# A hybrid decoder layer on one core: the sample's dilated attention and SSD moved into the output projection's Block

## The chip, the cores and the metric

The kernel runs on one core of a Trainium2 chip, as one launch. The metric is the device time of that core in microseconds (us), the median of several runs. Everything is float32; matrix products are made of three passes over a high and a low part of each operand.

## What is computed

One layer for a prompt of 2048 tokens and for a sample of 8 sequences with one new token each; both share the weights. Each token is projected, mixed by three mixers side by side, projected out with `w_out` and sent through a gated feed-forward part:

```python
def layer(x, rel_bias, ln_mix_w, w_in, ..., past=None):
    aq, ak, av, bq, bk, bv, logf, cz, cxbc, cdt = in_project(rmsnorm(x, ln_mix_w), w_in, fgate_b)
    ...
    a_out, win_new = dilated_decode(aq, ak, av, win_bufs, rel_bias)     # sample; dilated_prompt for the prompt
    b_out = fox_decode(bq, bk, bv, logf, fox_kv, fox_logf, page_table)
    c_out, h_new, conv_new = ssd_mixer(cz, cxbc, cdt, conv_buf, h0, conv_w, conv_b, dt_bias, A_log, D_skip, ssm_norm_w)
    x = x + jnp.concatenate([a_out, b_out, c_out], axis=-1) @ w_out
    f, ffn_new = conv_ffn(rmsnorm(x, ln_ffn_w), ffn_buf, w_up, ffn_conv_w, ffn_conv_b, w_down)
```

For the sample, the dilated attention has three groups of two heads. Each attends from one token to 128 cached rows at distance d, 2d, ... (d = 1, 4, 16) and to itself; the groups are merged by a softmax over their log-sums. The sample's SSD is a four-tap convolution, a silu, and for each head a state update `h = h * exp(dt*A) + (x*dt) B`, with `y = C h + D x`, a gate and an RMSNorm.

## The kernel before

`program` runs stages one after the other, each a Block of its own: all five engines meet at its end, and no engine starts the next stage earlier. The order is `project`, `fox_stage` (FoX attention of prompt and sample), `local_stage` (dilated attention and SSD of the prompt), `dilated_decode`, `ssd_decode` (the sample's), `out_project`, `channel_mixer`, `finish`. Between some of them `clear_semaphores` gives semaphores back. Inside a Block each engine runs its own list in order, and semaphores tie the lists together.

**`dilated_decode`** (line 2349) loads all own rows and all cache rows, then VectorE works through the groups (lines 2421 to 2432), GpSimd takes one maximum over all partitions (line 2407), ScalarE the exponentials, TensorE the sums over partitions with a matrix of ones (line 2474). SP stores one row and four statistics for each group to `ma` (line 2398).

**`ssd_decode`** (line 2479) puts the 8 sequences on 8 partitions for the convolution, writes B and C to memory and reads them back as twelve broadcasts over 64 partitions each (line 2543, `sd_bc`), updates the state in three parts (lines 2600 to 2607), stores it and writes a row to `mc`.

**`out_project`** (line 1538) takes 17 tiles of 128 tokens: tile 0 is the sample, tiles 1 to 16 are the prompt. It splits the eight chunks of `w_out` into high and low parts through two buffers, and computes for all tiles the shares of the dilated groups and the SSD's norm (lines 1735 to 1747). For each tile, SP loads the mix in three pieces from `ma`, `mb`, `mc` into one of two buffers (lines 1622 to 1624) and `x` (line 1627). GpSimd multiplies it by norm, weights and shares (lines 1657 to 1661). TensorE turns it in by 8 transposes (line 1810), ScalarE and VectorE split it (lines 1687, 1756), TensorE makes 48 products (lines 1836 to 1838) and turns the normalized previous tile out by 8 transposes (line 1817). VectorE adds the residual (line 1766), ScalarE and VectorE make the RMSNorm (square, root, three Newton operations, scale), VectorE weighs the result (line 1780, in the listings `op_h`), and ScalarE's queue stores `x2` and `h2` (lines 1693, 1702). The tiles run in a hardware loop of two tiles a trip (`over_pipeline`, line 1522); SP loads the mix of tile t+1 once tile t is turned in and its predecessor's residual is added:

```python
                    sp.wait_ge(m_turned, t + 1)
                    load(t + 1, 1 - slot)
                    sp.wait_ge(x2_ready, t + 1)
                    load_x(t + 1, 1 - slot)
```

Here `m_turned`, `x2_ready` start one ahead. `channel_mixer` begins with the load of `h2` (line 1970).

## Time and profile before

| | us |
|---|---|
| median of 3 runs | 3397.13 |
| lowest, highest | 3391.59, 3399.49 |
| the profiled execution | 3402.59 |
| its span, first to last instruction | 3399.9 |
| mean granted TensorE clock, share of full | 0.947 |

The profile records one execution. Its times count from the first instruction, and its pages name instructions by line, engine, operation and the tiles written and read. PE is TensorE, PEld its weight load, DVE VectorE, ACT ScalarE, POOL GpSimd, SP the engine that issues most DMAs (SPq its DMA issues, ACTq ScalarE's). Over the span TensorE is busy for 3028.7 us (89%), VectorE for 1605.9 (47%), ScalarE for 878.2 (26%), GpSimd for 757.8 (22%). The stages around the change are at these times: the dilated attention of the sample from 1409.57, its SSD from 1475.42, the output projection from 1546.79, the channel mixer from 1842.49.

### The profile page before, as it was taken

Reading aid. Unit: us, or ns where it says so; the run is one execution under the profiler, and the core shown is the slowest. Engines: PE = TensorE matmul, PEld = TensorE weight load, DVE = VectorE, ACT = ScalarE, POOL = GpSimd, SP = SyncE. Lnnn points to the kernel's source line nnn. Section 1 sums busy time; section 2 is a strip of 40 time slices with the busy share of each in tenths; the row PEclk is TensorE's granted clock in tenths of the full one; section 3 lists DMA queues with packets and bytes.
Section 4 is the critical chain, followed back from the end, with each engine's and each line's share of the span. In section 5 each row is a group of like instructions: output and inputs, shape, how many; then the busy total and the mean of one; then the engine's idle time right before and its main releaser. Section 6 shows DMA issues by size and latency. Waiting matters only on the chain. (4 is left out here: it accounts for less than half of the span.)

```text
span 3399.9 us, 45796 instructions
## 1 busy us (share of the span) xinstructions
PE 3028.7 (89%) x16539; PEld 2604.6 (77%) x16539; DVE 1605.9 (47%) x2952; ACT 878.2 (26%) x1647; POOL 757.8 (22%) x547
## 2 busy tenths in 40 slices
PE   8999999689998899413885999999999899999998
PEld 6888889677675899303774999999999788888886
DVE  5013211257775888443333455544555544444445
ACT  4223222233332455202222221112211322112212
POOL 4002100234442455201211112211221112211220
PEclk9999999889999999756997999999999999999999
DMA  4454325557762333434444311111111511111101
GB/s 152 169 205 163 103 91 173 136 167 207 200 193 89 91 91 98 122 67 122 142 147 182 111 37 59 53 37 37 44 56 50 186 37 50 61 38 37 62 25 51
DMA packets 227573, 352.16 MB, mean 104 GB/s; under 512 B 73502, under 2 KB 161175, under 8 KB 221448
## 3 DMA queue, kind: packets, MB, share of 16 engines
q1 hardware_dynamic: 221601, 310.06, 29.9%
q0 software_dynamic: 944, 22.61, 1.8%
q10 hardware_dynamic: 4896, 17.83, 1.3%
q8 instruction: 71, 1.16, 0.1%
q14 instruction: 61, 0.50, 0.0%
HBM read 285.64 MB, written 93.95 MB: 112 GB/s over the span
## 5 line engine op out<-in xcount | busy, mean ns | idle before, releaser
L2985 PE MATMUL pj_acc<-pj_w_hi,pj_h_hi 128*128 128x480 f32 (+5 forms) x952 | 356.6, 375 | 8.5 <-DVE pj_w_lo L2885 8.5
L2986 PE MATMUL pj_acc<-pj_w_lo,pj_h_hi 128*128 128x480 f32 (+5 forms) x952 | 355.6, 374 | 0.0
L2987 PE MATMUL pj_acc<-pj_w_hi,pj_h_lo 128*128 128x480 f32 (+5 forms) x952 | 354.9, 373 | 0.0
L2314 PE MATMUL cm_g_ps<-cm_h_hi,cm_up_hi 128*128 128x344 f32 (+1 forms) x880 | 310.0, 352 | 36.8 <-DVEq L2258 30.7
L2077 POOL TENSOR_TENSOR cm_dn_lo<-cm_dn_raw,cm_dn_hi 128x1024 fp32r<-128x1024 f32 x44 | 107.8, 2472 | 1000.5 <-ACT cm_dn_hi L2119 1000.5
L2314 PE MATMUL cm_u_ps<-cm_h_hi,cm_up_hi 128*128 128x344 f32 (+1 forms) x880 | 309.5, 352 | 2.7 <-DVE cm_a_lo L2218 2.7
L2316 PE MATMUL cm_g_ps<-cm_h_hi,cm_up_lo 128*128 128x344 f32 (+1 forms) x880 | 309.5, 352 | 0.0
L2316 PE MATMUL cm_u_ps<-cm_h_hi,cm_up_lo 128*128 128x344 f32 (+1 forms) x880 | 308.8, 351 | 0.0
L2315 PE MATMUL cm_g_ps<-cm_h_lo,cm_up_hi 128*128 128x344 f32 (+1 forms) x880 | 308.7, 351 | 0.0
L2315 PE MATMUL cm_u_ps<-cm_h_lo,cm_up_hi 128*128 128x344 f32 (+1 forms) x880 | 308.2, 350 | 0.0
L2885 DVE TENSOR_TENSOR pj_w_lo<-pj_w_raw,pj_w_hi 128x480 fp32r<-128x480 f32 (+3 forms) x112 | 76.3, 703 | 393.8 <-ACT pj_w_hi L2840 393.8
L2072 POOL TENSOR_TENSOR cm_up_lo<-cm_up_raw,cm_up_hi 128x2048 fp32r<-128x2048 f32 x44 | 205.0, 4659 | 193.9 <-ACT cm_up_hi L2099 193.9
L2182 DVE TENSOR_SCALAR cm_conv<-cm_gate,cm_small 128x344 f32<-128x344 f32 (+2 forms) x110 | 54.2, 493 | 334.7 <-ACT cm_gate L2112 192.4
L2314 PEld LDWEIGHTS cm_g_ps<-cm_h_hi,cm_up_hi 128*128 128x128 f32 x880 | 166.7, 189 | 53.3 <-issue 31.1
L371 POOL TENSOR_TENSOR fp_prod<-fp_kv,fp_q_own 128x1024 f32<-128x1024 f32 x64 | 151.4, 2366 | 226.9 <-DVE fp_s_dec L414 226.9
L2985 PEld LDWEIGHTS pj_acc<-pj_w_hi,pj_h_hi 128*128 128x128 f32 (+1 forms) x952 | 175.2, 184 | 34.3 <-issue 9.0
L2987 PEld LDWEIGHTS pj_acc<-pj_w_hi,pj_h_lo 128*128 128x128 f32 (+1 forms) x952 | 174.8, 184 | 25.7 <-issue 1.1
L2986 PEld LDWEIGHTS pj_acc<-pj_w_lo,pj_h_hi 128*128 128x128 f32 (+1 forms) x952 | 174.7, 183 | 24.9 <-issue 0.5
L2232 DVE TENSOR_TENSOR cm_y<-cm_y,cm_y_ps 128x1024 f32<-128x1024 f32 x99 | 120.9, 1221 | 137.5 <-PE cm_y_ps L2341 137.5
L2818 ACT ACTIVATE pj_row<-pj_acc,pj_rstd 128x480 f32<-128x480 f32 (+6 forms) x119 | 76.2, 641 | 409.0 <-PE pj_acc L2987 374.4
L2314 PEld LDWEIGHTS cm_u_ps<-cm_h_hi,cm_up_hi 128*128 128x128 f32 x880 | 165.9, 189 | 18.6 <-DVE cm_a_lo L2218 3.1
L2315 PEld LDWEIGHTS cm_g_ps<-cm_h_lo,cm_up_hi 128*128 128x128 f32 x880 | 166.6, 189 | 16.5
(431 smaller groups left out, 6538.0 us busy)
## 6 DMA issues: line engine op xcount, KB each, us to landing
fp_kv<-in_fox_kv SPq DMA_DIRECT2D x256, 256.0 KB, 3.0
cm_up_raw<-in_w_up SPq DMA_DIRECT2D x44, 1024.0 KB, 4.9
cm_dn_raw<-in_w_down SPq DMA_DIRECT2D x44, 512.0 KB, 3.5
out_s_win<-in_cache POOLq DMA_DIRECT2D x8, 2047.0 KB, 9.3
proj_a<-pj_row SPq DMA_DIRECT2D x48, 240.0 KB
sp_raw<-proj_b SPq DMA_DIRECT2D x16, 640.0 KB, 4.1
pj_w_raw<-in_w_a SPq DMA_DIRECT2D x10, 960.0 KB, 8.0
dp_raw<-proj_a SPq DMA_DIRECT2D x48, 192.0 KB, 3.4
```

What stands on the lines that cost most here:

```text
L371: pool.tensor_tensor(prod[:, n % 2], kv[:, at:at + QUART, 0], q_own[:, a // 2:a // 2 + 1].to_broadcast([P, QUART, F]), ALU.mult).then_inc( ...
L2072: pool.tensor_tensor(up_lo[:, s], up_raw[:, s], up_hi[:, s].bitcast(F32), ALU.subtract).then_inc(up_ready, 1)
L2077: pool.tensor_tensor(dn_lo[:, s], dn_raw[:, s], dn_hi[:, s].bitcast(F32), ALU.subtract).then_inc(dn_ready, 1)
L2232: v.tensor_tensor(y[:, n], y[:, n], sums(H, n).rearrange("p a n -> p (a n)"), ALU.add).then_inc(added, 1)
L2314: pe.matmul(out, hi, h_hi[:, k, cs], start=(k == 0), stop=False)
L2315: pe.matmul(out, hi, h_lo[:, k, cs], start=False, stop=False)
L2316: last = pe.matmul(out, lo, h_hi[:, k, cs], start=False, stop=(k == KT - 1))
L2818: act.activation(row[0:m, n % ROWS, 0:wide], acc[0:m, n % BANKS, 0:wide], ACT.Copy, scale=rstd[0:m, t:t + 1]).then_inc(evac, 1)
L2885: v.tensor_tensor(w_lo[:, j % 2, k, 0:n], w_raw[:, k, 0:n], w_hi[:, j % 2, k, 0:n].bitcast(F32), ALU.subtract).then_inc(w_ready, 1)
L2985: pe.matmul(out, h_hi[:, k, place(t)], w_hi[:, j % 2, k, 0:wide], start=(k == 0), stop=False)
L2986: pe.matmul(out, h_hi[:, k, place(t)], w_lo[:, j % 2, k, 0:wide], start=False, stop=False)
L2987: last = pe.matmul(out, h_lo[:, k, place(t)], w_hi[:, j % 2, k, 0:wide], start=False, stop=(k == KT - 1))
```

## The change

`dilated_decode`, `ssd_decode` and `over_pipeline` go. `out_project` becomes `out_stage`, one Block without a hardware loop, that also does the sample's two mixers. The semaphores are cleared between `local_stage` and `out_stage`.

- The tiles are written out in the order 1 to 16 and then 0. A *slot* is the piece of the program in which TensorE multiplies one tile: slot s has tile number s in that order, counted from 0; slots 0 and 1 are done together at the start, with the weight chunks as they come. A slot is divided by phases 1 to 9, and a step of the sample's work has an address `at(slot, phase)`. Each engine has two generators of steps (`dilated`, `ssd`) that it advances at its `until(slot, phase)`.
- There are three mix buffers and three weight buffers, and the mix of tile s+2 is loaded in slot s. Turn-in, split, turn-out and weighing are done in halves of four chunks. GpSimd uses the shares directly and makes three operations for a tile, without the two copies.
- All transfers of the stage are issued by SP, the stores of `x2` and `h2` too.
- The dilated groups are done one after the other with one set of buffers, from slots 2, 5 and 8 on, with one all-reduce each (three for one); the own rows are read as two broadcasts of 128 columns for each group, the own V as one row. The next group's loads wait for the store of the last group's result.
- The SSD's convolution runs on 128 partitions (16 for each sequence, 56 columns) after 26 small loads; all of it goes to memory and x comes back from there. The broadcasts go to two buffers: eight are issued in slot 5, four in slot 9. The state update runs in slots 7 to 12.
- The shares and norm of tile 0 are made at the end of slot 13, after the sample's results were stored.

```diff
+    ORDER = list(range(1, ALL_TILES)) + [0]
+    def group_slot(g):
+        return 2 + 3 * g
+    state_at = [[(7, 5), (7, 7), (7, 9), (8, 9), (9, 3)],
+                [(9, 5), (9, 9), (10, 3), (10, 5), (10, 7)],
+                [(11, 3), (11, 5), (11, 7), (11, 9), (12, 3)]]
...
         @block.sync
+            def load_mix(j):
+                if j >= 3:
+                    sp.wait_ge(m_turned, 2 * (j - 2))
...
+            def dilated():
+                for g in range(GROUPS):
+                    if g:
+                        yield at(group_slot(g) - 1, 9)
+                        sp.wait_ge(d_added, 2 * g)
+                        sp.wait_ge(d_stored, 32 * g)
+                    for k in range(2):
+                        sp.dma_start(d_own[:, :, k], bcast(pa.tensor, k * A_WIDTH + g * P, [[COLS_A, DEC], [1, P]])
+                                     ).then_inc(d_landed, 16)
+                    sp.dma_start(d_row[:], ...).then_inc(d_landed, 16)
+                    sp.dma_start(d_kv[:].rearrange("p b k c -> p b (k c)"), ...).then_inc(d_landed, 16)
+                    yield at(group_slot(g) + 2, 9)
+                    sp.wait_ge(d_added, 2 * g + 2)
+                    sp.dma_start(ma[0:DEC, g * P:(g + 1) * P]..., d_row[:]).then_inc(d_stored, 16)
...
+            load_w(0)
+            sp.dma_start(c_sum[:, 1:], ...).then_inc(sums_in, 16)
+            load_mix(0)
...
+            for s in range(1, N + 1):
+                until(s, 4)
+                if 3 <= s + 2 < LAST:
+                    load_mix(s + 2)
+                if s == SAMPLE_SLOT:
+                    sp.wait_ge(d_stored, 32 * GROUPS)
+                    sp.wait_ge(s_out, 16 * (XT + 3))
...
+                    load_mix(LAST)
+                if s >= 2:
+                    for j in residuals(s):
+                        sp.wait_ge(x2_ready, j + 1)
+                        sp.dma_start(x2_d[t * P:(t + 1) * P, :], x2[:, j % 2]).then_inc(x2_stored[j % 2], 16)
+                        if j + 2 < N:
+                            load_x(j + 2)
+                until(s, 6)
+                    for j in norms(s):
+                        sp.wait_ge(h2_ready, 2 * j + 2)
+                        sp.dma_start(h2_d[ORDER[j]], h2[:, j % 2]).then_inc(h2_stored[j % 2], 16)
+                until(s, 9)
...
         @block.gpsimd
+            for j in range(3):
+                mixing(j)
+            for s in range(1, N):
+                if 3 <= s + 2 < N:
+                    mixing(s + 2)
+                beside.until(at(s, 9))
...
         @block.vector
+            for s in range(2, N + 1):
+                for j in residuals(s):
+                    residual(j)
+                if s + 1 < N:
+                    split(s + 1, 0)
+                for n, j in enumerate(norms(s)):
+                    scale(j)
+                    if n == 0:
+                        until(s, 4)
+                        if s + 1 < N:
+                            split(s + 1, 1)
+                        until(s, 6)
+                    weigh(j, 0)
+                    until(s, 7)
+                    weigh(j, 1)
+                until(s, 9)
+                if s == SAMPLE_SLOT:
+                    factors_of(0, 1, 2)
...
         @block.tensor
+            for s in range(2, N):
+                if s + 1 < N:
+                    turn_in(s + 1, 0)
+                until(s, 1)
+                pe.wait_ge(m_ready, 2 * s + 2)
+                pe.wait_ge(x2_ready, s - 1)
+                multiply(s, 0, range(0, 4))
+                if s + 1 < N:
+                    turn_in(s + 1, 1)
+                until(s, 2)
+                multiply(s, 0, range(4, 8))
+                until(s, 5)
...
+                multiply(s, 1, range(0, 4))
+                if s != 3:
+                    turn_out(ends[-1], 0)
+                until(s, 8)
+                multiply(s, 1, range(4, 8)).then_inc(mm_done, 1)
...
+                turn_out(ends[-1], 1)
+                until(s, 9)
```

Three places in the engines' lists. The first is SP's DMA issues of one tile in the projection's loop (`mix_a`, `mix_b`, `mix_c` are the pieces of the mix, `op_x` the residual's input), before:

```order
L1622 DMA op_mix<-mix_a 128x384
L1623 DMA op_mix<-mix_b 128x256
L1624 DMA op_mix<-mix_c 128x384
L1627 DMA op_x<-in_x 128x1024
L1525 REGISTER_ALU
L1525 COMPARE_AND_BRANCH
```

and now, at the end of slot 4 and the start of slot 5 (`h` is the store of `h2`, `x` that of `x2`):

```order
L1790 DMA h<-op_h 128x1024
L1693 DMA mix_a<-dd_row 8x1x128
L1695 DMA mix_a<-dd_stat 8x1x4
L1685 DMA dd_own<-proj_a 128x8x128 x2
L1687 DMA dd_row<-proj_a 1x8x128
L1689 DMA dd_kv<-in_cache 128x8x256
L1718 DMA conv_rows<-sd_conv 128x56
L1659 DMA op_mix<-mix_a 128x384
L1660 DMA op_mix<-mix_b 128x256
L1661 DMA op_mix<-mix_c 128x384
L1783 DMA x<-op_x 128x1024
L1666 DMA op_x<-in_x 128x1024
```

Two stores and five transfers of the sample now stand ahead of the mix load of tile 7 (with a wait between the stores and the loads). The second place is VectorE's tile work in the loop, from the end of one tile's norm to the next tile's residual, before:

```order
L1519 TENSOR_TENSOR op_rstd<-op_rstd,op_tmp 128x1
L1780 TENSOR_TENSOR op_h<-op_tr_ps,op_lnw 128x1024
L1755 REGISTER_ALU
L1756 TENSOR_TENSOR op_m_lo<-op_in_ps,op_m_hi 128x1024
L1766 TENSOR_TENSOR op_x<-op_acc_ps,op_x 128x1024
L1769 TENSOR_SCALAR op_sq<-op_sq 128x1
```

and now in slot 5:

```order
L1519 TENSOR_TENSOR op_rstd<-op_rstd,op_tmp 128x1
L1990 TENSOR_TENSOR dd_prod<-dd_kv,dd_own 128x1024
L1923 TENSOR_TENSOR op_m_lo<-op_in_ps,op_m_hi 128x512
L1992 TENSOR_REDUCE dd_s<-dd_prod 128x16
L1977 TENSOR_TENSOR op_h<-op_tr_ps,op_lnw 128x512
L1994 SCALAR_TENSOR_TENSOR dd_s<-dd_s,dd_bias 128x16
L1998 TENSOR_TENSOR dd_prod<-dd_own 128x1024
L1977 TENSOR_TENSOR op_h<-op_tr_ps,op_lnw 128x512
```

The group's first product, which needs the cache rows, stands between the norm and both the second split and the first weighing. The third place is GpSimd around the sample's all-reduce (`dd_m`; a bare `ISA` is an instruction without named tiles), before:

```order
L2407 ISA dd_m<-dd_s 128x48
L2353 UNCONDITIONAL_BRANCH
L1645 UNCONDITIONAL_BRANCH
L1653 COPY op_share_now<-op_share 128x6
L1655 COPY op_c_now<-op_c_rstd 128x1
L1657 ISA
L1657 TENSOR_TENSOR op_mix<-op_mix,op_c_now 128x384
```

and now in slots 2 and 3:

```order
L1810 TENSOR_TENSOR op_mix<-op_mix,op_share 128x384
L1816 ISA
L1816 ISA dd_m<-dd_s 128x16
L1806 ISA
L1806 TENSOR_TENSOR op_mix<-op_mix,op_c_rstd 128x384
L1807 TENSOR_TENSOR op_mix<-op_mix,op_norm_w 128x384
```

The bare instruction ahead of a mix's first multiplication stood once, behind the one all-reduce; now it stands behind each of three, in the middle of the tiles, and not at the start of the stage.

## Rows read from the trace of the kernel before

**Rows 1.** Busy time by stretch; columns: stretch, length, engines (instructions), granted clock, DMA share, GB/s.
```profile
1409.50:1475.40 65.90, 9.66 (x22) 5.03 (x22) 26.94 (x33) 0.38 (x2) 0.50 (x1) 0.58 0.36 122
1475.40:1546.80 71.40, 1.90 (x12) 1.25 (x12) 33.70 (x37) 2.28 (x6) 0.00 (x0) 0.50 0.50 94
1600.00:1815.00 215.00, 192.46 (x932) 156.30 (x932) 68.12 (x149) 51.97 (x74) 40.90 (x70) 1.00 0.41 142
```

**Rows 2.** Timeline of both sample stages: start, length, engine, line, [idle before <- releaser].
```profile
1409.57 0.35 SPq L2388 DMA_DIRECT2D dd_ones<-in_consts  x1
...
1436.31 1.87 PE L2463 MATMUL dd_den_ps<-dd_rel,dd_onehot 32*128 32x6 f32 x8 [36.08 <-DMA dd_kv<-in_cache]
...
1473.37 0.62 SPq L2400 DMA_DIRECT2D mix_a<-dd_stat  x1
...
1475.42 0.36 SPq L2524 DMA_DIRECT2D sd_ident<-in_consts  x1
...
1491.23 1.08 DVE L2572 TENSOR_TENSOR sd_tmp<-sd_past,sd_taps 8x896 f32<-8x896 f32 x1
...
1503.62 12.46 SPq L2543 DMA_DIRECT2D sd_bc<-bc_rows  x12
...
1523.20 1.23 DVE L2600 TENSOR_TENSOR sd_upd<-sd_bc,sd_col 128x1024 f32<-128x1024 f32 x1 [18.18 <-DMA sd_bc<-bc_rows]
...
1544.44 0.30 SPq L2551 DMA_DIRECT2D mix_c<-sd_y  x1
```

**Rows 3.** DMA issues of the dilated stage and the projection: count, KB each, median us to landing.
```profile
dd_kv<-in_cache SPq DMA_DIRECT2D x3, 1024.0 KB, 18.9
...
dd_ones<-in_consts SPq DMA_DIRECT2D x1, 64.0 KB, 1.8
...
op_stats<-mix_a SPq DMA_DIRECT2D x1, 102.0 KB, 5.6
...
op_c_sum<-mix_c SPq DMA_DIRECT2D x1, 8.5 KB, 6.5
```

**Rows 4.** Timeline of the start of the output projection.
```profile
1546.79 0.84 SPq L1612 DMA_DIRECT2D op_w_raw<-in_w_out  x2
...
1550.70 1.06 ACT L1669 ACTIVATE op_w_hi<-op_w_raw 128x1024 fp32r<-128x1024 f32 x1 [6.28 <-DMA op_w_raw<-in_w_out]
...
1557.48 0.20 DVE L1735 TENSOR_TENSOR op_top<-op_stats 128x34 f32<-128x34 f32 x1 [2.58 <-DMA op_lnw<-in_ln_ffn]
...
1558.55 1.28 ACT L1675 ACT_TABLE_LOAD   x1
...
1561.76 0.18 DVE L1519 TENSOR_TENSOR op_c_rstd<-op_c_rstd,op_c_tmp 128x17 f32<-128x17 f32 x1
...
1569.05 0.82 POOL L1657 TENSOR_TENSOR op_mix<-op_mix,op_c_now 128x384 f32<-128x384 f32 x1 [6.73 <-issue]
...
1569.94 1.96 POOL L1658 TENSOR_TENSOR op_mix<-op_mix,op_norm_w 128x384 f32<-128x384 f32 x1
```

**Rows 5.** Timeline of one tile of the output projection's loop.
```profile
1611.78 1.09 PE L1810 MATMUL op_in_ps<-op_ident,op_mix 128*128 128x128 f32 x8 [1.82 <-POOL op_mix L1661]
...
1615.19 1.22 DVE L1766 TENSOR_TENSOR op_x<-op_acc_ps,op_x 128x1024 f32<-128x1024 f32 x1
...
1618.82 0.36 SPq L1624 DMA_DIRECT2D op_mix<-mix_c  x1
...
1623.12 0.19 POOL L1653 COPY op_share_now<-op_share 128x6 f32 x1 [11.39 <-DMA op_mix<-mix_c]
...
1623.91 1.03 PE L1817 MATMUL op_tr_ps<-op_ident,op_xn 128*128 128x128 f32 x8
...
1626.33 1.09 PE L1810 MATMUL op_in_ps<-op_ident,op_mix 128*128 128x128 f32 x8 [1.39 <-POOL op_mix L1661]
```

**Rows 6.** Timeline of the projection's end and the channel mixer's first load.
```profile
1830.07 1.22 DVE L1766 TENSOR_TENSOR op_x<-op_acc_ps,op_x 128x1024 f32<-128x1024 f32 x1
...
1842.49 0.33 SPq L1970 DMA_DIRECT2D cm_y<-h  x1
```

More of the change, by code:

```diff
@@ L1665, in _ @@
+            beside = Beside(dilated())
+            for j in range(3):
[4 more added lines that the diff above has]
+                beside.until(at(s, 9))
         @block.scalar
@@ L1847 @@
+            turn_out(LAST, 0)
+            turn_out(LAST, 1)
 class Half:
```

1079 lines of the change are left out of this document (559 added, 520 removed).

## Prediction

> **What bounds the kernel now.** I read the busy time by stretch first [rows 1]. Between 1409.5 and 1546.8 us, TensorE is busy for 9.66 and 1.90 us; from 1600 to 1815 us it is busy for 192 of 215. So the two sample stages leave the bounding engine almost idle, while the output projection nearly fills it. The timeline [rows 2] says what they wait for. The dilated attention starts at 1409.57, and nothing computes before 1436.31, when its loads have landed. The SSD starts at 1475.42 and has a second gap until 1523.20, while twelve broadcasts come back from memory. It stores its last row at 1544.44, and the projection issues its first load at 1546.79. These stages are serial: every microsecond in them is on the path.
>
> In the projection, one tile of the loop [rows 5] shows the pace. A turn-in starts at 1611.78, the next at 1626.33, 14.55 us later. TensorE idled 1.39 of that for GpSimd, which waited for the mix: issued at 1618.82, used at 1623.12, 4.3 us. The tile's own TensorE work is 14.55 - 1.39 = 13.16 us. That is at the full clock (granted 1.00, the level of 2.4 GHz [rows 1]).
>
> **The change, part by part.** The sums are made on the profiled execution, 3402.6 us (span 3399.9). The median of the runs is 3397.1, 5.5 less.
>
> Removed: the two stages, 1546.79 - 1409.57 = 137.2 us. The semaphore clearing stays, now between the local stage and the new one. Its cost is bounded by two changes of stage [rows 2]: last issue to first issue is 2.4 us with it (1544.44 to 1546.79) and 2.05 without (1473.37 to 1475.42). I take 0.6 us. **Gain 136.6.**
>
> Start of the stage. Let T be its first load. Before, tile 1's residual add is at 1615.19 = T+68.4 [rows 4, 5]. Now the factor sums are issued third, at about T+0.9, and land 6.5 us later [rows 3]: T+7.4. VectorE's chain of factors took 1557.48 to 1561.94, 4.5 us: T+11.9. GpSimd's three multiplications for tile 0 follow. Before, GpSimd stood 6.73 us ahead of the first of them with nothing waited for [rows 4]. The order shows an unnamed GpSimd instruction there, between the all-reduce and the first ordinary operation, and none at the start of the new stage, which comes from ordinary operations. I take those 6.7 us as gone here; if they are not, the start is 6.7 later. The multiplications took 4.7 us beside VectorE's work (the second 1.96 [rows 4]). Tile 0 is mixed at about T+16.5, tile 1 at T+20, both turned in and split at T+23. From there TensorE multiplies two tiles, 24.3 us by turn-in start to turn-out start (1623.91 - 1611.78 = 12.13, twice [rows 5]), plus an estimated 1.5 at the lower clock. Three weight buffers instead of two keep ahead of it: six products of a chunk for each tile hold 2.8 us, and one round of a buffer is 3.9 us of loading (1546.79 to the first split at 1550.70 [rows 4]) and two splits of 1.06 and 1.23 us, 6.2 us in all, shared by three buffers. Tile 1's residual: T+49.5. **Gain 68.4 - 49.5 = 18.9**, 12 to 23.
>
> Fifteen further tiles. Before: 1615.19 to 1830.07, 214.9 us [rows 5, 6]. Now the mix is fetched two tiles ahead, so TensorE's own 13.16 sets the pace: 15 x 13.16, less the last tile's absent turn-in (0.9, by the 1.03 of the turn-out's eight), is 196.5. The sample adds its TensorE work, at most 9.66 + 1.90 [rows 1], partly at the lower clock there; I take 9. Together 205.5. **Gain 9.4** before any stall. The tail, 1830.07 to 1842.49 [rows 6], is the same chain: 0, or 1 better by its halves.
>
> VectorE takes the sample's work on board: 26.9 + 33.7 us before [rows 1]. The convolution's nine operations, 896 columns on 8 partitions at 1.08 us or more [rows 2], are now 56 columns on 128 partitions, so about 49 us remain, mostly in full-size operations of 1.23 us [rows 2]. Its own tile work is 68.1 us in 215, 4.6 us of 14.55. With up to five sample operations in a slot it is at 9 to 12 of 13.2 us: hidden by capacity, not always by order.
>
> **Stalls, the disputed term.** All transfers now leave by SP's queue in written order. Group 1's four loads are issued at the end of slot 4 (order rows), behind a wait until the group 0 row is stored. Let S be the moment TensorE begins slot 5. SP arrives at S+0.8, stores h2, row and statistics (0.6 each) by S+2.4, waits 2 us for landing (1473.37 to 1475.42 [rows 2]), and has the loads out between S+4.4 and S+6. Their transfer: two own-row broadcasts of 0.5 MB in 512-byte pieces and 1 MB of cache. Twelve such broadcasts of 0.25 MB took 1503.62 to 1523.20, so 1 MB takes about 6 us; the four large loads of the dilated stage, 7.7 MB, took 1409.57 to 1436.31 with all else, so 1 MB takes about 3. Landed: S+15. VectorE waits for that in the middle of tile work: behind it are the second half-split (tile 6), a sum and the first half-weighing of tile 4 (order rows), 3.8 us. TensorE wants that weighing at S+12.7 and gets it at S+19. The mix of tile 7 is behind the same loads and lands at S+17; GpSimd needs 2.7 more, TensorE wants it at S+13.2. Both say **6 to 7 us lost, for group 1 and again for group 2** (slot 8): 14. Group 0 loads under the start.
>
> Does a load wait behind others? The table of transfers [rows 3]: 64 KB alone took 1.8 us, 102 KB issued behind 1 MB of weights took 5.6. The Trainium skill, "DMA: Bandwidth & Descriptors", section "Queues, rings and completion order", says that each DMA engine consumes the descriptors of one issuing engine's ring in order. By that rule the mix pays for every sample load issued ahead; without it, only the wait of VectorE would remain.
>
> Then the echoes. The all-reduce of each group is followed by the 6.7 us reload ahead of the next mix; in slots 5 and 8 the mix is already late, so the next one is due at S+38 against S+33, 4.5 us. In slots 6 and 9 the eight and four broadcasts add to that. I take half, 4 in all. VectorE's order in slots 8 to 10, the wait for yT in slot 12 and the sample's factors in slot 13 cost 1 to 2 us each; I take 4. **Stalls 22**, bounded by 0 (all landings in time) and 45 (every one in full).
>
> **Sum:** 3402.6 - 136.6 - 18.9 - 9.4 + 22 = 3259.7, at the median 3254.
>
> **Rivals.**
> *Hidden:* the loads land by the time they are asked for, and the reload fits the two tiles of slack. For it: DMA share is only 0.41 during the loop [rows 1]. Against it: the SP's wait on its own store. It gives 3254 - 22 = 3232.
> *Clogged:* all stalls in full, or VectorE's order binds slots 3 to 12; also exponentials between square roots need ten more table loads of 1.28 us [rows 4] inside the chain that ends in the turn-out, which has 1 to 2 us to spare. It gives 3254 + 23 = 3277. The Trainium skill, "ScalarE: Activation LUTs", section "What ACT_TABLE_LOAD costs", gives 2.66 us a switch with its drain; the load's row here is 1.28. By the page, five reloads ahead of a square root would cost 7 more, 3284.
> *Slower than before:* each of the 15 slots waits for a landing. dd_kv took 18.9 us to land where it was queued [rows 3]. If every mix took that instead of 4.3, a slot would be 4.3 + 9 + 3 us late after 4 us of slack; slots would have to average (137 + 28) / 15 = 11 us more than now planned for the gain to be gone. That needs about 3 MB ahead of every mix; the sample has some 12 MB in all, enough for four slots, so 3410 is nearly out.
> *It doesn't overlap:* a wait makes slot 5 or 8 hold until the sample is done, the old loads' latency back on the path (27 + 18 us): 3254 + 45 = 3299.
>
> **How the numbers follow.** Forecast 0.50, hidden 0.25, clogged 0.20, not overlapping 0.03, slower 0.02. A measurement of this kernel can tell a change of 0.2%, 7 us, from none; every case but the last is far outside that. The range takes the forecast with its start term (12 to 23), reaches below hidden (3226) and to clogged (3282). Faster 0.97, same 0.01, slower 0.02.
>
> **What would show it.** The stage, from first SP load to the channel mixer's first, should last 289 us (267 if hidden). Tile 1's residual add at T+49; ordinary slots 13.2 us apart, and slots 5 to 6 and 8 to 9 near 20, with VectorE idle for dd_kv and GpSimd idle for the mix there. GpSimd should show no 6.7 us gap at the start and one after each all-reduce. I am wrong if a residual interval is above 22, if all are 13 to 14, or if the start is above T+56.

## The result and the profile after

| | before | after |
|---|---|---|
| median of four runs each, us | 3398.31 | 3268.61 |
| lowest, highest | 3391.59, 3407.48 | 3264.48, 3271.63 |
| profiled execution, its span | 3399.9 | 3269.8 |
| mean granted clock | 0.947 | 0.962 |

The ratio is 0.9616, with a 95% interval of 0.9589 to 0.9642: 130 us faster. The forecast was 3254, so it was 15 us too low, with its range (3226 to 3282) holding the time; the rival "clogged" (3277) is nearer to the result than the forecast is. The interesting question is where those 15 us are.

The new stage, first load to the channel mixer's first load, took 1719.13 - 1418.17 = 301.0 us. The prediction said 289. The first lines are the timeline after at the points that answer [rows 4 and 6]; columns as there.

```profile
1418.17 0.38 SPq L1747 DMA_DIRECT2D op_stats<-mix_a  x1
...
1425.41 1.28 ACT L1855 ACT_TABLE_LOAD   x1
...
1429.64 0.83 POOL L1806 TENSOR_TENSOR op_mix<-op_mix,op_c_rstd 128x384 f32<-128x384 f32 x1 [26.51 <-DMA op_lnw<-in_ln_ffn]
...
1466.00 2.34 DVE L1959 TENSOR_TENSOR op_x<-op_acc_ps,op_x 128x1024 f32<-128x1024 f32 x2
...
1707.14 1.21 DVE L1959 TENSOR_TENSOR op_x<-op_acc_ps,op_x 128x1024 f32<-128x1024 f32 x1
...
1719.13 0.33 SPq L2374 DMA_DIRECT2D cm_y<-h  x1
```

The line at 1466.00 holds the residual adds of tiles 0 and 1; the second begins at 1467.13, T+49.0 (predicted T+49.5, before T+68.4). GpSimd's first operation waits for a transfer only, with no gap without a releaser [rows 4]. The tail is 12.0 us (12.4 before [rows 6]). So start and tail came as forecast, and the fifteen tiles between took 240.0 us, not 227.5.

Below, "slot s" is the time from the residual add of tile s-1 to that of tile s. Slots 12, 15 and 16 are left out of the table (12.9, 13.0 and 12.1 after); the runs are those of the next section. Without sample work (e1) an ordinary slot lasts 12.9 or 13.0.

| slot | 2 | 3 | 4 | 5 | 6 | 7 | 8 | 9 | 10 | 11 | 13 | 14 | stage |
|---|---|---|---|---|---|---|---|---|---|---|---|---|---|
| after | 15.3 | 19.2 | 17.1 | 21.4 | 14.7 | 18.4 | 21.9 | 15.5 | 14.0 | 14.4 | 16.3 | 13.9 | 301.0 |
| e1, no sample | 13.6 | 16.2 | 13.0 | 12.9 | 13.0 | 12.9 | 13.0 | 12.9 | 13.0 | 12.9 | 16.3 | 14.0 | 263.6 |
| e3, early loads | 15.2 | 19.8 | 16.9 | 14.5 | 14.9 | 21.0 | 15.6 | 17.0 | 14.0 | 14.4 | 16.3 | 12.5 | 291.0 |
| e9, mix earlier | 15.2 | 19.5 | 17.2 | 20.9 | 15.1 | 17.4 | 21.7 | 15.5 | 14.0 | 14.4 | 16.3 | 14.1 | 300.1 |
| e10, four edits | 15.3 | 19.9 | 15.3 | 14.0 | 15.1 | 16.8 | 15.6 | 17.1 | 16.0 | 14.4 | 12.9 | 13.0 | 284.1 |
| e11, six edits | 15.9 | 17.0 | 18.7 | 13.3 | 14.3 | 16.0 | 14.3 | 16.1 | 14.9 | 13.8 | 13.0 | 13.9 | 280.6 |
| e12, last | 15.9 | 14.2 | 16.9 | 13.4 | 14.1 | 16.0 | 14.3 | 16.1 | 14.9 | 13.8 | 11.9 | 13.9 | 273.8 |

Slot 5 is the place the prediction spoke of most. Its timeline after (SP, VectorE, GpSimd and TensorE together):

```profile
1517.89 0.60 PE L2131 MATMUL op_in_ps<-op_ident,op_mix 128*128 128x128 f32 x4
...
1519.90 0.63 SPq L1695 DMA_DIRECT2D mix_a<-dd_stat  x1
1521.85 1.00 SPq L1685 DMA_DIRECT2D dd_own<-proj_a  x2
...
1523.59 0.53 SPq L1689 DMA_DIRECT2D dd_kv<-in_cache  x1
...
1527.98 0.61 SPq L1661 DMA_DIRECT2D op_mix<-mix_c  x1
...
1532.30 1.22 DVE L1990 TENSOR_TENSOR dd_prod<-dd_kv,dd_own 128x1024 f32<-128x1024 f32 x1 [8.71 <-DMA dd_kv<-in_cache]
...
1532.83 8.13 SPq L1729 DMA_DIRECT2D sd_bc<-conv_rows  x8
...
1533.89 0.83 POOL L1806 TENSOR_TENSOR op_mix<-op_mix,op_c_rstd 128x384 f32<-128x384 f32 x1 [24.76 <-DMA op_mix<-mix_c]
...
1536.24 1.09 PE L2140 MATMUL op_tr_ps<-op_ident,op_xn 128*128 128x128 f32 x4 [5.67 <-DVE op_h L1977]
...
1542.25 0.42 SPq L1659 DMA_DIRECT2D op_mix<-mix_a  x1
...
1543.05 0.39 POOL L1816 PARTITION_ALL_REDUCE dd_m<-dd_s  x1 [6.47 <-issue]
```

TensorE began slot 5 at S = 1517.89, its turn-in. SP waited for the store from 1520.5 to 1521.85, the cache left at S+5.7 and landed at S+14.4 (predicted S+15). VectorE stood 8.71 us for it in the middle of its tile work. TensorE got its half-weighing at S+18.3 (predicted S+19) and waited 5.67 us. Slot 8 shows the same: 8.52 us on VectorE, 4.88 on TensorE.

What the prediction did not have is what follows such a pause. Busy time by stretch, columns as in [rows 1]; the clock is the figure behind the five engines:

```profile
1495.00:1500.00 5.00, 2.02 (x12) 1.52 (x12) 2.19 (x6) 1.15 (x1) 1.65 (x2) 0.92 0.01 2
1500.00:1505.00 5.00, 3.63 (x7) 2.16 (x7) 3.66 (x9) 1.95 (x4) 0.00 (x0) 0.50 0.79 247
1505.00:1510.00 5.00, 5.00 (x23) 4.04 (x22) 4.02 (x10) 3.15 (x4) 3.58 (x3) 0.90 0.50 175
1530.00:1536.20 6.20, 0.57 (x3) 0.13 (x1) 3.84 (x5) 0.00 (x0) 2.23 (x3) 0.77 1.06 374
1536.20:1541.00 4.80, 4.76 (x17) 4.17 (x18) 4.55 (x6) 0.60 (x1) 0.38 (x1) 0.59 1.21 193
...
1583.00:1589.00 6.00, 1.59 (x7) 0.94 (x5) 3.41 (x4) 0.00 (x0) 1.95 (x3) 0.91 0.88 336
1589.00:1594.00 5.00, 4.53 (x15) 3.98 (x16) 4.75 (x7) 0.60 (x1) 0.66 (x1) 0.50 0.30 102
1594.00:1599.00 5.00, 3.76 (x17) 2.79 (x17) 3.23 (x10) 1.42 (x4) 0.39 (x1) 0.93 0.73 228
```

(TensorE's waits in these slots are 0.91, 2.62, 0.88 and 1.37 in slot 3, 5.67 in slot 5, 0.97 and 4.88 in slot 8: 17.3 us.) In three places TensorE was busy for 2.02 of 5, 0.57 of 6.2 and 1.59 of 6 us, and in the 5 us behind each it worked with a granted clock of 0.50 to 0.59, which is the level of 1.2 GHz for nearly all of the stretch. Busy time times what the clock lacks, 3.63 x 0.50 + 5.00 x 0.10 + 4.76 x 0.41 + 4.53 x 0.50 + 3.76 x 0.07, is 6.8 us of work done slower.

Not every pause is followed by it. These are the wait of 3.03 us in slot 7 and that of 2.74 us in slot 13 of the kernel after, each with the stretch behind it, and then the stretch behind the same wait of slot 13 (2.75 us) in e3:

```profile
1550.00:1555.20 5.20, 2.17 (x13) 1.57 (x11) 4.89 (x9) 0.00 (x0) 3.86 (x3) 1.00 0.53 200
1555.20:1560.00 4.80, 4.80 (x24) 3.56 (x25) 2.46 (x5) 3.12 (x5) 1.69 (x2) 1.00 0.93 307
...
1665.00:1670.20 5.20, 2.46 (x12) 1.70 (x11) 4.14 (x17) 2.96 (x5) 1.90 (x3) 0.96 0.25 102
1670.20:1675.00 4.80, 4.80 (x17) 4.00 (x18) 1.64 (x7) 2.21 (x5) 0.72 (x1) 0.68 0.65 218
```

```profile
1653.80:1658.60 4.80, 4.80 (x23) 3.98 (x24) 1.64 (x7) 2.28 (x5) 0.78 (x1) 1.00 0.62 218
```

So slot 13 has a fourth slow stretch, 4.80 x 0.32 = 1.5 us, 8.3 us in all. Behind waits of about 3 us the clock went either way: it stayed whole in slot 7 here and in e5 (3.26 us), and fell to 0.66 behind 3.16 us in e7. The 1.4 us by which slot 14 is shorter in e3 and e4 (12.5) than here (13.9) are of this size, with the same wait ahead. What decides it no run here shows.

One caution on totals. Outside the stage the code is the same, but its time is not: span less stage is 2968.8 us in this execution and 2954.3 to 2967.8 in those of e1 and e3 to e12; before, without the two sample stages and the projection, it is 2967.0. The local stage's last transfer is issued at 1402.29 before, at 1410.67 after, and between 1395.86 and 1405.76 in the first four runs below (1405.76 with the old sample stages kept). So an execution can be 15 us longer for reasons that have no place in the change, and I read each edit in its slots and its stage first.

### The profile page after: what moved, and what is told of

Read it like the earlier page. It is cut to its first block and busy times, and to the rows that moved or that the text cites. A ratio compares the mean times of both kernels' runs of the same rounds, so it can differ in the third digit from the quotient of the medians.

```text
span 3269.8 us, 45453 instructions
## 1 busy us (share of the span) xinstructions
PE 3033.6 (93%) x16543; PEld 2605.8 (80%) x16543; DVE 1604.0 (49%) x2998; ACT 892.5 (27%) x1680; POOL 757.2 (23%) x515
## 3 DMA queue, kind: packets, MB, share of 16 engines
q8 instruction: 78, 1.28, 0.2%
## 5 line engine op out<-in xcount | busy, mean ns | idle before, releaser
L2720 PEld LDWEIGHTS cm_g_ps<-cm_h_hi,cm_up_lo 128*128 128x128 f32 x880 | 166.3, 189 | 16.0
```

The costliest lines, as they stand in the source:

```text
L2720: last = pe.matmul(out, lo, h_hi[:, k, cs], start=False, stop=(k == KT - 1))
```

## Experiments

Each starts from the changed kernel, unless it says otherwise. "Theory" is that of its text, which was written before it ran.

### e1: the stage without the sample's work

The sample's steps are left out on all engines:

```
-            beside = [Beside(dilated()), Beside(ssd())]
+            beside = []
+            sp.dma_start(mc[0:DEC], mc[P:P + DEC]).then_inc(s_out, 16)
+            sp.dma_start(ma[0:DEC], ma[P:P + DEC]).then_inc(d_stored, 16)
```

> All of the sample's dilated attention and SSD is left out of the stage; rows of tile 1 are copied in memory in their place. My theory (the stalls come from the sample's loads, waits and reloads; the unrolled order alone runs at 13.16 us a tile): the stage lasts 301.0 - 34 (stalls) - 9 (TensorE work) = 258 us, all residual intervals 13 to 14, total 3268.6 - 43 = 3226. Rival (the unrolled order itself stalls, in slots 2 to 4 above all, where two tiles are normed one after the other): slots 2 to 4 stay at 15, 19 and 17, the stage lasts 266 or more, total 3234 or more.

Measured: 3224.2 us, ratio 0.9473 (0.9457 to 0.9489); stage 263.6. The total came as expected (3226), the stage lies between the two theories (258 and 266). The start took 0.9 us more, the rest of the 5.6 us is in three slots: 16.2 for slot 3, where two tiles are normed one after the other, and 16.3 and 14.0 for slots 13 and 14. In slot 13 VectorE has the sample tile's factors between its last weighing and the next residual add, and ScalarE has their exponential, a table load and their square root ahead of its next split:

```profile
1617.88 0.15 DVE L1941 TENSOR_TENSOR op_top<-op_stats 128x2 f32<-128x2 f32 x1
...
1618.68 1.28 ACT L1860 ACT_TABLE_LOAD   x1
...
1620.09 0.58 ACT L1843 ACTIVATE op_m_hi<-op_in_ps 128x512 fp32r<-128x512 f32 x1
...
1621.23 1.23 DVE L1966 TENSOR_TENSOR op_x<-op_acc_ps,op_x 128x1024 f32<-128x1024 f32 x1
...
1623.20 1.09 PE L2140 MATMUL op_in_ps<-op_ident,op_mix 128*128 128x128 f32 x4 [2.73 <-DVE op_m_lo L1930]
```

(This is e1's timeline.) The 1.1 us of slot 14 are the clock again, 0.65 in the 4.8 us behind that wait. So the unrolled order has 5.3 us of its own over the 196.5 of the prediction (201.8 for fifteen slots), although its plain slots are 0.2 faster than 13.16. And all the sample's work costs the stage 301.0 - 263.6 = 37.3 us.

### e2: the sample's stages kept ahead of the unrolled projection

```
+        dilated_decode(nc, pa, ...)        # as in the kernel before
+        ssd_decode(nc, pb, ...)
         clear_semaphores(nc, kept)
-        out_stage(...)
+        out_stage(...)                     # with beside = []
```

> The sample's two stages stand ahead of the projection as before the change; the projection is the unrolled one with the sample's tile last, with no sample work in it. My terms: 3402.6 - 18.9 (start) - 18.4 (15 tiles at 13.16) = 3365 profiled, 3360 median. Rival (the unrolled order stalls by itself): 3372 or more. On the 8.4 us by which the local stage ended later after the change: if the length of the program's code ahead or behind does it, this kernel shows it too (last load issue of the local stage near 1410); if it is one execution's chance, it may stand anywhere between 1402 and 1411.

Measured: 3362.2 us, ratio 0.9880 (0.9863 to 0.9896); stage 262.7. By the medians the unrolled order alone is worth 39 us (the theory said 37) and the overlap another 94. The stretch from the local stage's last transfer to the channel mixer's first load is free of the rest of the program: 440.2 us before, 407.4 here, 308.5 after, so 33 and 99. The 4 us that 33 lacks of 37 are the order's own stalls, as in e1. The local stage's last transfer was issued at 1405.76.

### e3: the group's loads a slot earlier

```
-                    if g:
-                        yield at(group_slot(g) - 1, 9)
-                        sp.wait_ge(d_added, 2 * g)
-                        sp.wait_ge(d_stored, 32 * g)
-                    for k in range(2):
-                        sp.dma_start(d_own[:, :, k], ...)
-                    sp.dma_start(d_kv[:]..., caches[g]...)
+                    if g + 1 < GROUPS:
+                        yield at(group_slot(g) + 1, 9)
+                        sp.wait_ge(d_weighed, g + 1)
+                        group_loads(g + 1)      # d_own x2 and d_kv
```

(`d_row` keeps its place and gets a semaphore of its own.)

> Groups 1 and 2: the two broadcasts of own rows and the cache are issued at the end of slots 3 and 6, as soon as VectorE has read the last of the group before, instead of slots 4 and 7 behind the store of its row; the row itself is fetched where it was. My theory (the store and the late landing cost slots 5 and 8): intervals of 21.4 and 21.9 us fall to 14 to 15, total 3268.6 - 14 = 3255. Rival (any transfer of 2 MB delays the mix behind it wherever it is issued): slots 3 or 4 and 6 or 7 grow by what slots 5 and 8 lose, total 3265 to 3272.

Measured: 3248.1 us, ratio 0.9548 (0.9532 to 0.9564); stage 291.0. Slots 5 and 8 fall by 6.9 and 6.3 us, 13.2 together, while TensorE's two waits there were 5.67 and 4.88: the rest is the clock, 1.00 in the stretches that were at 0.59 and 0.50. So the late loads were the cause, and their place is right. But 2.6 us came back in slot 7 and 1.5 in slot 9. In slot 7 TensorE waits 4.19 us for a mix that was issued behind the eight broadcasts (the next group's loads follow only later), in slot 9 2.43 us for VectorE's split, and behind both the clock is 0.66. By the medians e3 is 20 us faster than the kernel after, by the stage 10; its profiled execution is 12 us or more longer than its three others, so I take the stage.

### e4: the mix ahead of the group's loads

```
-                        yield at(group_slot(g) - 1, 9)
+                        yield at(group_slot(g), 5)
```

> Groups 1 and 2: all their loads are issued in slots 5 and 8 behind the mix and the stores of x2, instead of ahead of them. If VectorE's wait in the middle of tile work is what binds (my theory), it waits some 4 us longer and the total is 3268.6 + 2 x 4 = 3277. Rival (the mix that stands behind the loads binds): GpSimd's mix is in time again, slots 5 and 8 fall by 4 to 7 us each, total 3255 to 3261.

Measured: 3268.5 us, ratio 0.9625 (0.9597 to 0.9653); stage 307.4. GpSimd had its mix 3.7 us after its last part was issued, and it helped nothing: VectorE now waits 14.72 us and TensorE 11.69 in slot 5, which grows to 27.0, slot 8 to 24.6. That is 8.2 us more in the two, as the theory said (8); the stage grows by 6.5 only, since slots 7 and 14 are 1.0 and 1.4 shorter. The total doesn't show it, and the forecast of 3277 missed: in the profiled execution the rest of the program took 2954.3 us, the least of all runs, so 6.5 us are below what it can tell. VectorE's wait binds here, and the mix behind the loads does not.

### e5: no reduction on GpSimd

```
-                    pool.partition_all_reduce(d_m..., d_s..., P, RMAX).then_inc(d_topped, 1)
+                    pool.tensor_tensor(d_m[:], d_s[:], d_s[:], ALU.mult).then_inc(d_topped, 1)
```

> GpSimd's reduction over partitions (the maximum of the scores) is replaced by one ordinary multiplication of the same 128x16 tile, so the maximum is wrong and the sample's attention with it; nothing else changes. My theory (the reload of 6.5 to 8 us ahead of and behind each reduction makes the mix late in slots 3, 6 and 9, the echo): GpSimd shows no wait of 6 us or more without a releaser, and the stage of 301.0 us is 4 to 6 shorter. Rival (the mix of those slots is late for its loads anyway, and GpSimd's reload hides in that wait): less than 2 us. Other rival (every reload is paid in full): 15 or more.

Measured: 3261.4 us, ratio 0.9584 (0.9568 to 0.9600); stage 302.3, 1.3 more than after. ("Reload" is the name here and in the prediction for the time without a visible releaser beside the reduction; what GpSimd does in it no trace shows.) The reloads are gone, and no slot is more than 0.1 us shorter; the median is 7 us lower, which no slot accounts for. My theory fell: alone, the reload costs nothing.

### e6: the broadcasts of B and C behind the next mix

```
-                yield at(5, 5)
+                yield at(5, 9)
                 sp.wait_ge(s_bounced, 16)
                 sp.dma_start(s_x[:], bounce_d[:, 0:C_INNER]).then_inc(s_x_in, 16)
+                yield at(6, 5)
```

> The wait for the bounced convolution rows and the load of x move from the middle of slot 5 to its end, and the eight broadcasts of B and C (8.1 us of issuing) from there to slot 6 behind the mix of tile 8. My theory: the mix of tile 8, which GpSimd waited for until 1551.2, comes 6 us or more earlier, the interval of 18.4 us falls to 15 to 16, the stage to 297 or 298. Rival (GpSimd's reload after its reduction sets that mix, or the broadcasts are now late for VectorE in slot 7 instead): no change within 1 us, or longer.

Measured: 3264.0 us, ratio 0.9595 (0.9579 to 0.9611); stage 304.2. Slot 7 grew from 18.4 to 20.9: TensorE waits 3.97 us for the mix instead of 3.03, and behind it works for 5 us at a granted clock of 0.66, 1.7 us more. The broadcasts, issued from 1530.82, took SP 9.96 us. This is GpSimd and TensorE in slots 6 and 7 of e6:

```profile
1531.02 0.39 POOL L1817 PARTITION_ALL_REDUCE dd_m<-dd_s  x1 [5.78 <-issue]
1541.12 0.82 POOL L1807 TENSOR_TENSOR op_mix<-op_mix,op_c_rstd 128x384 f32<-128x384 f32 x1 [9.71 <-issue]
...
1544.80 0.66 PE L2132 MATMUL op_in_ps<-op_ident,op_mix 128*128 128x128 f32 x4 [3.97 <-POOL op_mix L1811]
```

and the same place in e5, without the reduction:

```profile
1540.18 1.03 POOL L1806 TENSOR_TENSOR op_mix<-op_mix,op_c_rstd 128x384 f32<-128x384 f32 x1 [14.53 <-DMA op_mix<-mix_c]
...
1544.18 0.66 PE L2130 MATMUL op_in_ps<-op_ident,op_mix 128*128 128x128 f32 x4 [3.26 <-POOL op_mix L1810]
```

With the mix landed, the reload of 9.71 us makes it late; with no reload, the landing does. Each covers the other, so that either alone can be removed without gain. (That in e6 the mix had landed is read from its issue by 1529.5 and from GpSimd's wait, which names no transfer.)

### e7, e8: one of the two mixers left out

```
e7:           def ssd():
+                return
e8:           def dilated():
+                return
```

> The sample's SSD is left out (rows of tile 1 stand in for its result in memory); the dilated attention stays. The whole sample work costs 301.0 - 263.6 = 37.3 us of the stage. By the intervals, slots 9 to 12 and the broadcasts are the SSD's: 5 + 4 us. My theory: the stage falls by 10, to 291, intervals of 19 and 21 us in slots 4, 5 and 8 staying. Rival (the two mixers hold each other up on VectorE and SP, so that one alone is nearly hidden): it falls by 20 or more.

> The sample's dilated attention is left out (rows of tile 1 stand in for it); the SSD stays. My theory: it carries 27 of the 37 us, the stage falls to 274. Rival (the two hold each other up): it falls to 268 or less, while leaving out the SSD alone gives 20 or more too.

Measured: stages 297.2 and 277.1 us (3262.9 and 3236.8 in one run each). Without the SSD the stage falls by 3.8, without the dilated attention by 23.9; 27.7 together, of 37.3. Both theories missed, and so did the rivals. Slot by slot, the 10 us between 27.7 and 37.3 are three things. In slot 7 (18.4, 17.5, 17.2 and 12.9 with both, without the SSD, without the attention, with none) each mixer alone costs nearly what both do: 3.4 us. Slots 3 and 8 add 0.8 and 1.0 in the same way, and slot 4 takes 1.2 back. The other 6.0 are new stalls of the two reduced kernels: slot 10 is 16.0 in e7, against 14.0, and slot 11 is 18.8 in e8, against 14.4. In slot 11 of e8 TensorE waits for a mix that stood behind four broadcasts in SP's order:

```profile
1586.36 0.66 PE L2136 MATMUL op_in_ps<-op_ident,op_mix 128*128 128x128 f32 x4 [2.63 <-POOL op_mix L1812]
```

(The granted clock from 1585 to 1590 is 0.72.) So leaving work out can move a stall instead of removing it, and the differences of such runs are not the two mixers' shares. In e7, too, TensorE waits in slot 7, 3.16 us, behind the reload.

### e9: each mix fetched one slot earlier

```
-                if 3 <= s + 2 < LAST:
-                    load_mix(s + 2)
+                if s + 3 < LAST:
+                    load_mix(s + 3)
```

(and `load_mix(3)` behind the weights)

> Each mix is fetched one slot earlier (its buffer is free by then): tile s+3 in slot s instead of tile s+2. The reduction's echo and the broadcasts were each worth nothing alone. My theory now: they cover each other (with no SSD TensorE still waits 3.16 us for GpSimd in slot 7, then behind the reload; with no reduction 3.26, then behind the landing), and the earlier fetch removes both: slot 7 falls from 18.4 to 14 or 15, no wait of TensorE for GpSimd's mix above 0.5 us remains. Slots 5 and 8 are bound by VectorE's wait for the cache and stay at 20 to 22. Stage 296 to 297. Rival (slot 7 is bound by something else, such as TensorE's own sample work): stage 300 to 302. Rival (the mix behind the group's loads binds slots 5 and 8 as well): stage below 290.

Measured: 3263.6 us, ratio 0.9619 (0.9603 to 0.9636); stage 300.1, which is what the first rival said. In this one point the theory holds: of TensorE's waits for GpSimd's mix only the one at the start is left. But slot 7 fell to 17.4 only. Two things remain in it. The sample's own work on TensorE is large there: two pairs of 1.02 us for the weighted sums and 0.72 for nine transpositions, 2.8 us; and TensorE waits 2.29 us for VectorE's row work ahead of one of the sums. So three causes lay on top of each other in slot 7, of which the prediction knew two.

### e10: four edits together

Those of e3 and e9, and:

```
-                yield at(3, 4)                     # VectorE: convolution
+                yield at(4, 4)
-                yield at(3, 7)                     # ScalarE: exp, tanh of the SSD
+                yield at(4, 7)
-                    yield at(group_slot(g) + 1, 5) # ScalarE: exp of the scores
+                    yield at(group_slot(g) + 1, 5 if g else 8)
...
                     norm(j)
                     if n == 0:
+                        if s == SAMPLE_SLOT + 1:
+                            factors_of(0, 1, 2)
...
-                if s == SAMPLE_SLOT:
-                    factors_of(0, 1, 2)
```

(The steps that hang on these follow: VectorE's and TensorE's of group 0, and the SSD's on VectorE in slot 4. TensorE's weighted sums also move, for all groups, from phase 1 to phase 2 of their slot.)

> Four edits together, each with its own place: the group's loads a slot earlier (slots 5 and 8), the mix a slot earlier (slot 7), the exponentials, tanh and convolution of the sample moved out of the double norm of slot 3 (slots 3 and 4), and the sample tile's factors moved into slot 14 behind its residual add (slots 13 and 14). My theory: slot 3 falls from 19.2 to 16.5 (the 16.2 without sample), slot 4 from 17.1 to 14 to 15 because the clock stays up, slots 5 and 8 to 14.5, slot 7 to 14.5, slot 13 from 16.3 to 13.5 and 14 from 13.9 to 13. Stage 301 - 2.7 - 2.5 - 7 - 7 - 4 - 3.5 = 274, total 3242. Rival (the clock of slot 4 falls in any case, or the work moved makes another slot late): stage 282 or more.

Measured: 3237.6 us, ratio 0.9535 (0.9519 to 0.9551); stage 284.1. Slots 5, 13 and 14 came as the theory said or better (14.0, 12.9 and 13.0), slot 8 near it (15.6 for 14.5), which settles what they were bound by. The stage did not (274; the rival said 282 or more), nor did slot 7 (16.8 for 14.5) and slot 3: 19.9, with only one table load left in it and that one behind the second norm. Slots 3 to 10 now show waits of TensorE of 0.4 to 2.45 us for VectorE's split. Slot 3 in e10:

```profile
1483.01 1.06 ACT L1856 ACTIVATE op_xn<-op_x 128x1024 f32<-128x1024 f32 x1 [4.35 <-PE op_tr_ps L2152]
...
1484.67 0.17 DVE L1515 RECIPROCAL op_rstd<-op_root 128x1 f32<-128x1 f32 x1 [0.33 <-ACT op_root L1858]
1484.87 0.86 DVE L1516 TENSOR_TENSOR op_tmp<-op_rstd 128x1 f32<-128x1 f32 x1
1485.77 0.75 DVE L1517 TENSOR_TENSOR op_tmp<-op_tmp,op_sq 128x1 f32<-128x1 f32 x1
...
1488.13 0.66 PE L2152 MATMUL op_tr_ps<-op_ident,op_xn 128*128 128x128 f32 x4 [2.42 <-ACT op_xn L1860]
```

The second norm can begin only when the first one's rows have been turned out of the one buffer `xn` (4.35 us), and its chain of 5.1 us is longer than the products that TensorE has left.

### e11: the turn-out of tile 2 in slot 4, the split ahead of the residual add

```
                 if s + 1 < N:
                     turn_in(s + 1, 0)
+                if s == 4:
+                    turn_out(2, 0)
...
                 multiply(s, 0, range(0, 4))
+                if s == 4:
+                    turn_out(2, 1)
...
VectorE:
+                if s > 2 and s + 1 < N:
+                    split(s + 1, 0)
                 for j in residuals(s):
                     residual(j)
```

> The four edits of the run before, whose slot 3 stayed at 19.9 us though no exponential stood between its two norms any more, and two further ones: the turn-out of tile 2, for whose scaled rows TensorE waited 2.42 us, moves from the end of slot 3 into slot 4 behind the first products; and VectorE splits the next tile ahead of its residual add. My theory now (slot 3 is bound by one norm after the other through a single buffer, and each pause of TensorE of some microseconds is followed by a stretch at a granted clock of 0.66; TensorE's waits of 0.9 to 2.45 us for VectorE's splits in slots 3 and 6 to 10 come from the residual add ahead of them): slot 3 falls from 19.9 to 14 to 15, slot 4 stays at 15 to 16 with the turn-out, slots 6 to 10 lose 5 to 8 in all. Stage 284.1 - 5 - 6 = 273, total 3227. Rival (TensorE's own sample work and its lower clock are what is left): stage 279 or more.

Measured: 3239.2 us, ratio 0.9527 (0.9511 to 0.9543); stage 280.6. Slots 6 to 10 lost 4.9 us, the least that was expected. The stage is in the rival's range (279 or more). Slot 3 fell to 17.0 only, since the pause had moved: TensorE now waited 3.30 us for the exponentials of group 0, which e10 had put behind the second norm, and the clock of slot 4 was 0.92.

### e12: those exponentials back, the SSD's last transposition later

```
-                    yield at(group_slot(g) + 1, 5 if g else 8)
+                    yield at(group_slot(g) + 1, 5)
-                yield at(12, 5)
+                yield at(12, 8)
                 pe.wait_ge(s_yT_in, 1)
```

(TensorE's and VectorE's steps of group 0 follow to their old places.)

> As the run before, but the exponentials of group 0 stand between the two norms of slot 3 again, as after the change, so that the sum of its weights needs no waiting (TensorE waited 3.30 us for them at the end of slot 3); and the transposition of the SSD's result moves from the middle of slot 12 to its end (a wait of 1.89 us). My theory (with the turn-out of tile 2 in slot 4 nothing on TensorE hangs on the second norm of slot 3, so the table loads there cost nothing; the pause and the clock behind it go together): slot 3 falls from 17.0 to 14, slot 4 from 18.7 to 15.5 to 16.5, slot 12 from 14.5 to 13. Stage 280.6 - 3 - 2.5 - 1.5 = 273.6, total 3231. Rival (the exponentials delay the second norm and with it the turn-out in slot 4, the pause only moves): slot 4 at 18 to 20, stage 278 or more.

Measured: 3233.9 us, ratio 0.9512 (0.9498 to 0.9526); stage 273.8 against 273.6 in the text. Slot 3 is 14.2, slot 4 16.9, slot 12 13.6. Between the start and the end TensorE's clock is whole. The row covers 1455 to 1668 us in e12, columns as in [rows 1]; the second is from 1467.20 to 1707.10 in the kernel after:

```profile
1455.00:1668.00 213.00, 204.74 (x994) 162.53 (x993) 128.97 (x271) 70.42 (x116) 41.03 (x39) 1.00 0.63 194
```

```profile
1467.20:1707.10 239.90, 212.38 (x990) 168.48 (x989) 129.90 (x271) 70.56 (x116) 40.32 (x42) 0.95 0.57 174
```

VectorE, ScalarE and GpSimd do the same work in both; TensorE's is 7.6 us shorter, as the same instructions ran at the upper level (8.3 by the four stretches above). Its longest wait here is 1.74 us. This version leaves nothing out and is 35 us faster than the changed kernel by the medians, 27 by the stage.

## Why the prediction was right, and where it was off

**The removed stages and the start.** Both as stated. From the local stage's last transfer to T it is 7.5 us (7.28 before), and 6.7 to 7.4 in the runs e1 and e3 to e12, so the clearing of semaphores is not to be told from nothing; the text had 0.6. The start was at T+49.0 against T+49.5, with no reload of GpSimd. e2 prices the unrolled order alone: 33 us by its stretch and 39 by the medians, where the prediction's terms give 18.9 + 18.4. In e2 the start gives 19.3 and the fifteen tiles 13.2.

**The fifteen tiles.** The term of 13.16 us a tile was right to 0.2 us (12.94 in e1), and TensorE's sample work was 9.4 us (9 in the text):

```profile
1467.00:1707.00 240.00, 8.21 (x19) 3.15 (x19) 4.63 (x10) 0.95 0.57 174
...
1467.00:1707.00 240.00, 1.21 (x12) 0.81 (x12) 0.76 (x2) 0.95 0.57 174
```

(the kernel after, instructions on `dd_o_ps` alone and on `sd_t_ps` alone; first figure behind the length: TensorE.) What the term lacked was the order's own stalls: 3.3 us in slot 3, 3.4 and 1.1 in slots 13 and 14. The text had counted 1 to 2 us for the factors and nothing for the double norm.

**The stalls, 22 in the text.** By the same sum they are 240.0 - 205.5 = 34.5 us: 5.3 of the order alone (201.8 - 196.5), and 240.0 - 201.8 - 9 = 29.2 of the sample. Set against plain slots of 12.95, and with TensorE's own sample work taken out, they lie as follows.

| slots | us in the text | us measured |
|---|---|---|
| 2 to 4 | 0 | 9.4 |
| 5 and 8, groups 1 and 2 | 14 | 17.4 |
| 6, 7 and 9, the echoes | 4 | 5.3 |
| 10 to 14, orders and factors | 4 | 5.3 |
| plain slots 0.2 faster than 13.16 | 0 | -3.1 |

(The last 0.2 to 34.5 is TensorE's sample work beyond 9.)

Groups 1 and 2: their chain, store, landing, VectorE's wait, was right link by link, and e3 gives 13.2 of the 17.4 back. That this is so near to 14 is in part luck. TensorE's two waits were 5.67 and 4.88, 10.6 us where 6 to 7 each had been priced, and the slower work behind them, 4.5 us, made up for it. The mix behind the same loads, named in the same sentence as a second cause, costs nothing while VectorE's wait stands (e4).

The echoes: slot 7 alone was 5.5 us over a plain slot, 2.8 of it TensorE's own work; its other 2.7 have three causes, each of which hides the others (e5, e6, e9). The size was near, the reading of it as one cause, GpSimd's reload, was not.

The step that failed is the term for slots 2 to 4, where the prediction had nothing ("Group 0 loads under the start"). They were 12.7 us over plain slots; 3.4 of that is TensorE's own sample work, which is in the 9, and 9.4 are stalls. The order alone makes 4.0 of them (e1: 16.2 for slot 3, the double norm), the sample 5.4. Group 0's and the SSD's steps fall together with the double norm there: slots 3 and 4 are 3.0 and 4.1 us over e1, own work included, and of these 7.1 us 4.3 remain without the SSD (e7) and 2.4 without the dilated attention (e8). With the turn-out of tile 2 moved out of slot 3 and the splits ahead (e12), the two slots lost 5.2 us.

And every stall was priced at its wait, as if TensorE went on at full clock behind it. The 8.3 us of work done slower are a part of the measured column, 2.3 in slots 3 and 4, 4.5 in slots 5, 8 and 9, 1.5 in slot 14. The prediction had granted the lower clock 1.5 us at the start and none later, though [rows 1] showed 0.58 and 0.50 wherever TensorE idled.

**The rivals.** "Hidden" (3232) is out: the waits are real. Nothing like 3299 or 3410 came up. The truth, 3268.6, is between the forecast and "clogged" (3277), nearer to the latter: that rival's VectorE order in slots 3 to 12 was partly right. Its table loads were not, but for one. From tile 1's residual add to the last, TensorE waits for ScalarE's scaled rows only once, 2.62 us in slot 3, and there a load of 1.28 us stands in the chain. In e10 no load stands there, but GpSimd slows the same chain by 1.3 us (below) and the wait is 2.42, so the load's part of it is not shown alone. Two loads stand between the two norms of slot 3 in e12, where the turn-out no longer hangs on the second norm, and the slot is 5.0 us shorter than after. Where one stands ahead of a square root, VectorE waits 1.36 us for the root and 0.33 where none does, as at 1522.65 and 1543.00 of the kernel after:

```profile
1522.65 0.17 DVE L1515 RECIPROCAL op_rstd<-op_root 128x1 f32<-128x1 f32 x1 [1.36 <-ACT op_root L1847]
...
1543.00 0.16 DVE L1515 RECIPROCAL op_rstd<-op_root 128x1 f32<-128x1 f32 x1 [0.33 <-ACT op_root L1847]
```

So a load ahead of a root cost the chain 1.0 us: the load took 1.28, and 0.28 of it lay beside VectorE's step. The figure that the Trainium skill gives, 2.66 us ("ScalarE: Activation LUTs", section "What ACT_TABLE_LOAD costs"), is not seen here.

On the order of a queue: the mix of tile 7 was used 3.7 us after its last part was issued with nothing large ahead (e4), 5.9 behind the group's loads (after), and the mix of tile 8 7.7 us behind eight broadcasts (after: 1543.55 to 1551.20). That agrees with what the Trainium skill says in "DMA: Bandwidth & Descriptors", "Queues, rings and completion order", but shared bandwidth would look the same, and no run had a second queue to tell them apart.

**The stated signs.** Stage 289: 301. Ordinary slots 13.2: 12.9 and 13.0 where nothing of the sample is. Slots 5 and 8 near 20: 21.4 and 21.9. One reload after each reduction: two of three are seen (8.5 and 7.1 us), the third lies under a wait for the mix; and one of 5.9 to 8.0 us ahead of each as well, which the text did not list. "Wrong if above 22, or all 13 to 14, or start above T+56": none, though 21.9 is 0.1 from the first.

## What to carry to other kernels

Price a stall of TensorE with what can follow it: here its waits in the fifteen tiles were 26.8 us, and work at a lower clock in four stretches behind them added an estimated 8.3. The waits of 4.9 and 5.7 us were each followed by such a stretch, waits of 2.7 to 3.3 us only in some runs. When work is laid beside a loop, look first at the places where the loop itself is already out of its rhythm (a double norm, a last tile's factors): here the slots around the double norm, priced at nothing, were the largest miss. And where taking one cause away gives nothing, look whether a second stands right behind it before calling the first harmless: the reload and the late landing were each worth 0 alone. Fetching one slot earlier removed both waits, and then showed a third behind them, so that the slot gained only 1.0 us.

## What was not expected of the hardware

GpSimd needs a time with no visible releaser ahead of its reduction over partitions as well as behind it: 5.9 to 8.0 us ahead in the kernel after, and 7.1 and 8.5 (up to 10.2, in e10) behind.

```profile
POOL dd_m L1816 <- issue: 20.4, 3, 8.0
...
POOL op_mix L1806 <- issue: 15.7, 2, 8.5
```

(the waits from 1400 to 1715 us in the kernel after: total, times, longest.) In e5, which has an ordinary operation in its place, neither line is there.

VectorE's smallest operations are not immune to GpSimd: the two of one column in e10 at 1484.87 and 1485.77 took 0.86 and 0.75 us, each ending with a multiplication of GpSimd, and 0.16 elsewhere:

```profile
1484.70 1.01 POOL L1818 TENSOR_TENSOR op_mix<-op_mix,op_norm_w 128x384 f32<-128x384 f32 x1
1485.67 0.83 POOL L1821 TENSOR_TENSOR op_mix<-op_mix,op_share 128x384 f32<-128x384 f32 x1
```

They stand in the norm's chain, so GpSimd's work beside them put 1.3 us on it.

And the same code of the fox and local stages ended up to 15 us apart from one execution to the next (last local transfer issued at 1395.86 to 1410.67). What makes the difference there stays open; no run varied it.
